# Two attention products in quarters of TensorE, and the delta rule's products on halves of the weight columns

## The chip, the cores and the metric

The program runs on one core of a Trainium2 chip. A time is the device time of one execution in microseconds (us). The matrix engine is TensorE, the others are VectorE, ScalarE and GpSimd; SyncE issues most of the DMAs. In the rows of the profile they are PE (with PEld for loads of weights), DVE, ACT, POOL and SP. A matrix product on TensorE loads weights of up to 128 rows by 128 columns and then streams up to 512 columns of the other operand past them, into one of eight PSUM banks of 128 partitions by 512 values.

## The reference, cut to what matters

All data are float32. A block of one model is followed by a block of another, on 1024 tokens of width 1024. The two parts that matter are the neighbourhood attention of the first block and the gated delta rule of the second.

```python
scores = jnp.einsum('bhrnqd,bhrnikd->bhrnqik', q_blk, kg).astype(jnp.float32)
scores = scores + bias[None]
scores = jnp.where(valid[:, :, None, :], scores, -1e30)
probs = jax.nn.softmax(scores, axis=(-2, -1)).astype(v.dtype)
out = jnp.einsum('bhrnqik,bhrnikd->bhrnqd', probs, vg)
...
t_mat = jnp.eye(CHUNK, dtype=jnp.float32) + bc[..., :, None] * dec_strict * kk
w_mat = lax.linalg.triangular_solve(t_mat, (bc * eG)[..., None] * kc, left_side=True, lower=True,
                                    unit_diagonal=True)
u_v = lax.linalg.triangular_solve(t_mat, bc[..., None] * vc, left_side=True, lower=True,
                                  unit_diagonal=True)
...
def step(S, xs):
    w_c, uv_c, qd_c, intra_c, kt_c, gl_c = xs
    u = uv_c - jnp.einsum('bhck,bhkv->bhcv', w_c, S)
    o = jnp.einsum('bhck,bhkv->bhcv', qd_c, S) + jnp.einsum('bhij,bhjv->bhiv', intra_c, u)
    S = jnp.exp(gl_c)[..., None, None] * S + jnp.einsum('bhck,bhcv->bhkv', kt_c, u)
    return S, o
```

The attention has 8 heads of width 64 on a grid of 16 rows by 64 tokens; a row attends to 8 rows, 512 keys. The delta rule has 8 heads of width 64, runs in both directions over 256 context tokens and then 1024 others.

## The kernel before, in words

Every engine has its own list of instructions, written out in order. They wait for each other through counters: each producer ticks one, and a consumer waits for a count. PSUM is a ring of eight banks (`Banks`): `bk.open(key, ...)` takes the next bank for a product, `bk.vacant` waits until its former content is gone, `bk.full` until it is filled, `bk.clear` until it is emptied. An order that is opened is the order in which the banks go round.

*First attention* (`tensor_natt`, `vector_natt`, `scalar_natt`, `gpsimd_natt`, L577 to L674). There are 64 items, one for a row of 64 tokens and a pair of heads j; head s of the pair lies on partitions 64s to 64s+63 of queries and keys. The queries `QB` are block-diagonal: an area of 128 partitions by 2 x 64 columns, zero where the head doesn't match, so that one product of 128 rows by 128 weight columns by 512 keys gives the scores of both heads (L591). VectorE adds the bias (L632) and takes the negative maximum (L636), ScalarE does the exponential with its sum (L659), VectorE the reciprocal (L641), GpSimd scales the row (L674), TensorE turns it in four transposes (L600), ScalarE copies that out of PSUM (L667), and TensorE multiplies it with the values, eight products with 64 weight columns, each head on its half of the output partitions (L617). VectorE copies the result out as a high and a low part (L647, L649). On TensorE item i's scores stand ahead of item i-3's transposes and item i-4's value products; ScalarE does the exponential of i and then the copy of i-3. Scores live in 2 buffers, exponentials in 5, turned ones in 3. The queries' copy from PSUM (`vector_query_out`, L512) is one instruction per head, and GpSimd zeroes `QB` beforehand (L559).

*Delta rule* (`tensor_delta` and its like, L2530 to L2640). It runs in rounds n of 128 tokens, dd being the direction. Each round's triangular matrices (8 heads, 2 directions) are inverted: diagonal blocks of 32 by 32 on VectorE in 30 steps (L2241, L2244), for round n+1 while round n's chain runs; out by DMA, one copy turned on ScalarE (L2252), and in again as `Y0` and `YT`. Blocks are then joined to 64 (`tensor_join_a`, L2286, `tensor_join_b`, L2309) and to 128 (`tensor_join_c` to `e`, L2330, L2348, L2366). The state's chain is: keys times state (`tensor_step_a`, L2388), residual on VectorE (L2398, L2400), the inverse times the residual (`tensor_step_b`, L2410), scaling on VectorE (L2418), queries times state (L2436), the state's product (`tensor_step_c`, L2445), output (`tensor_step_o`, L2458), the state's sum on VectorE (L2477). The next round's blocks of the matrix (L2176) leave by SyncE's DMAs (L2199) and return, half of them turned on ScalarE (L2220), before VectorE begins their inverse (L2237). In L2286, L2309, L2410 and L2458 the weights are 128 by 128 and 64 columns stream; in L2445 128 stream, of which the diagonal 64 by 64 parts are used. A float32 product is two instructions of weights and two of streaming.

## Time and profile before

| | |
|---|---|
| median of 3 runs | 3741.59 us (3739.25 to 3743.46) |
| the profiled execution | 3733.37 us, of which the span of instructions 3731.6 us |
| TensorE busy | 3562.2 us, 95% of the span |
| VectorE, ScalarE, GpSimd busy | 1847.5, 1186.6 and 704.0 us |
| granted TensorE clock, mean | 0.981 |
| first attention | about 165 to 322 us |
| delta rule, rounds | about 1936 to 2316 us |

A time in a row is from the start of the span. In a timeline a row is a run of like instructions of one engine: start, length of the run, engine, line, operation, operands, how many, and in brackets how long the engine was idle before it and what ended that. A granted clock of 1 is 2.4 GHz, 0.5 is 1.2 GHz.

### The profile page before, as it was taken

The numbers are of one execution on the slowest core, as the hardware profiler recorded it, in microseconds if no ns is written. First come the engines' busy times: TensorE is split into PE (matmuls) and PEld (weight loads), VectorE is DVE, ScalarE is ACT, GpSimd is POOL, SyncE is SP. The second block draws the span as 40 slices with busy tenths as digits, with TensorE's granted clock in tenths as the row PEclk, the third lists the DMA queues.
The fourth block names the chain that finished last, engine by engine and source line by source line (L and its number), as shares of the span: only waits on it lengthen the run. The fifth ranks groups of instructions, "written<-read, shape, count | busy, mean of one in ns | idle before, by whom it ended". The sixth has DMA issues, their size and how long they took to land. (4 is left out here: it accounts for less than half of the span.)

```text
span 3731.6 us, 46421 instructions
## 1 busy us (share of the span) xinstructions
PE 3562.2 (95%) x18318; PEld 2764.2 (74%) x18318; DVE 1847.5 (50%) x3351; ACT 1186.6 (32%) x2087; POOL 704.0 (19%) x532
## 2 busy tenths in 40 slices
PE   7999999999999999999988988988999999999998
PEld 6756778887888888875557877546788478888886
DVE  4276993213676555335578884669211142322322
ACT  3155772212311111234434553138211032111210
POOL 1163000010101111010020110129101113333333
PEclk9999999999999999999999998999999999999999
DMA  3100111112233232123012214000122111111111
GB/s 134 37 2 22 44 40 51 54 55 87 75 106 96 91 105 93 46 78 125 1 22 41 39 38 138 27 1 2 35 74 59 54 57 46 51 51 46 49 53 46
DMA packets 266342, 211.67 MB, mean 57 GB/s; under 512 B 65680, under 2 KB 231184, under 8 KB 265744
## 3 DMA queue, kind: packets, MB, share of 16 engines
q1 hardware_dynamic: 264368, 201.61, 17.4%
q10 hardware_dynamic: 1760, 7.08, 0.9%
q8 instruction: 149, 2.44, 0.3%
q14 instruction: 65, 0.53, 0.0%
HBM read 185.33 MB, written 21.50 MB: 55 GB/s over the span
## 5 line engine op out<-in xcount | busy, mean ns | idle before, releaser
L95 PE MATMUL ps<-halves 128*128 128x512 f32 x10408 | 2406.7, 392 | 19.1 <-DVE halves L1542 6.6
L95 PEld LDWEIGHTS ps<-halves 128*128 128x128 f32 x10408 | 1956.1, 188 | 441.4 <-issue 26.9
L95 PE MATMUL ps<-arena 128*128 128x512 f32 (+1 forms) x880 | 361.7, 564 | 11.2 <-issue 6.4
L1521 POOL TENSOR_TENSOR tmps<-tmps 128x512 f32<-128x512 f32 x128 | 143.7, 1123 | 981.4 <-ACT tmps L1489 981.4
L1542 DVE TENSOR_TENSOR halves<-tmps,halves 128x512 fp32r<-128x512 f32 x128 | 88.1, 691 | 435.4 <-ACT halves L1497 435.4
L1425 ACT ACTIVATE halves<-raws 128x2048 fp32r<-128x2048 f32 x62 | 118.3, 1909 | 556.0 <-PE ps L95 532.5
L95 PEld LDWEIGHTS ps<-arena 128*128 128x128 f32 x880 | 165.7, 193 | 170.3 <-issue 159.3
L1528 POOL TENSOR_TENSOR arena<-arena 128x512 f32<-128x512 f32 x128 | 164.8, 1294 | 191.3 <-DVE arena L1569 191.3
L1489 ACT ACTIVATE tmps<-ps 128x512 f32<-128x512 f32 x128 | 76.6, 598 | 363.9 <-PE ps L95 360.0
L1569 DVE TENSOR_TENSOR arena<-ps,arena 128x512 f32<-128x512 f32 x128 | 87.8, 690 | 194.9 <-PE ps L95 188.7
L1365 DVE SCALAR_TENSOR_TENSOR arena<-arena,sc 128x128 f32<-128x128 f32 x448 | 164.1, 366 | 15.9
L1432 DVE TENSOR_TENSOR halves<-raws,halves 128x2048 fp32r<-128x2048 f32 x62 | 142.0, 2290 | 55.3 <-ACT halves L1425 55.3
L95 PE MATMUL ps<-arena,tokens 128*128 128x512 f32 (+1 forms) x384 | 140.2, 523 | 0.0
L2943 POOL TENSOR_SCALAR arena<-arena,wst 128x640 f32<-128x640 f32 (+1 forms) x64 | 119.0, 1873 | 89.8 <-DVE wst L2897 89.7
L1559 DVE TENSOR_TENSOR arena<-arena,ps 128x512 f32<-128x512 f32 x128 | 85.2, 683 | 99.7 <-PE ps L95 99.7
L674 POOL TENSOR_SCALAR arena<-arena,sm 128x512 f32<-128x512 f32 x64 | 100.1, 1565 | 176.1 <-DVE sm L641 176.1
L2116 POOL TENSOR_TENSOR arena<-arena 128x512 f32<-128x512 f32 x40 | 44.5, 1140 | 455.0 <-PE ps L95 232.5
L1497 ACT ACTIVATE halves<-tmps 128x512 fp32r<-128x512 f32 x128 | 81.0, 633 | 154.5 <-POOL tmps L1521 154.5
L95 PEld LDWEIGHTS ps<-arena,tokens 128*128 128x128 f32 x384 | 72.4, 191 | 62.2 <-issue 59.2
L2244 DVE TENSOR_TENSOR arena<-arena 64x30 f32<-64x30 f32 (+5 forms) x300 | 103.9, 346 | 10.3
L2241 DVE TENSOR_TENSOR arena<-arena 64x30 f32<-64x30 f32 (+5 forms) x300 | 102.9, 343 | 10.0
L1093 POOL TENSOR_TENSOR valw<-valw,arena 128x512 f32<-128x512 f32 x8 | 14.0, 1748 | 444.3 <-DVE arena L1076 444.3
(306 smaller groups left out, 3532.3 us busy)
## 6 DMA issues: line engine op xcount, KB each, us to landing
raws<-in_w_ff SPq DMA_DIRECT2D x31, 1024.0 KB, 6.5
raws<-in_w_mlp SPq DMA_DIRECT2D x31, 1024.0 KB, 5.4
mixw<-in_w_in SPq DMA_DIRECT2D x56, 512.0 KB, 3.8
arena<-in_w_ada SPq DMA_DIRECT2D x48, 512.0 KB, 3.9
arena<-in_w_in SPq DMA_DIRECT2D x5, 2048.0 KB, 11.9
arena<-in_x SPq DMA_DIRECT2D x8, 1024.0 KB, 8.3
h_stash<-arena SPq DMA_DIRECT2D x1, 5120.0 KB, 30.0
inverses<-arena ACTq DMA_DIRECT2D x20, 256.0 KB, 2.9
```

The lines of the kernel that those rows point to most:

```text
L95: ins = e.matmul(out_ap, l, r, start=i == 0, stop=i == n - 1)
L674: e.tensor_scalar(pbuf[i % 5], pbuf[i % 5], c[:, 2:3], None, ALU.mult).then_inc(*a_sl.tick())
L1365: e.scalar_tensor_tensor(out=a, in0=raw_a[:, kk, :], scalar=sc3[:, kk, b:b + 1], in1=a, op0=ALU.mult, op1=ALU.add).then_inc(*(m_part if kk ...
L1425: e.activation(RR[:, FW + q * 4096:FW + q * 4096 + 2048], raw_of(n), ACT.Copy).then_inc(*f_wh.tick())
L1432: e.tensor_tensor(RR[:, FW + q * 4096 + 2048:FW + q * 4096 + 4096], raw_of(n), RR[:, FW + q * 4096:FW + q * 4096 + 2048].bitcast(F32), ALU ...
L1521: e.tensor_tensor(tt, tt, tt, ALU.mult).then_inc(*f_sq.tick())
L1528: e.tensor_tensor(dst, dst, tmg[(i * 8 + t) % 2], ALU.add).then_inc(*f_ad.tick())
L1542: e.tensor_tensor(fl[:, m, n0:n0 + N], ftmp[x % 2], fh[:, m, n0:n0 + N].bitcast(F32), ALU.subtract).then_inc(*f_fl.tick())
L1569: e.tensor_tensor(tmg[x % 2], bk.tile(key)[:, :], G2[:, nh * 512:nh * 512 + 512], ALU.mult).then_inc(*bk.emptying(key))
L2241: e.tensor_tensor(T3, bc(W3[:, k:k + 1, k + 1:32], [64, k, 31 - k]), bc(W3[:, 0:k, k:k + 1], [64, k, 31 - k]), ALU.mult).then_inc(*dv.tick())
L2244: e.tensor_tensor(W3[:, 0:k, k + 1:32], W3[:, 0:k, k + 1:32], T3, ALU.add).then_inc(*(i_sol if k == 30 else dv).tick())
L2943: ins = e.tensor_scalar(p, p, w4[i % 4][:, 6 + s:7 + s], None, ALU.mult)
```

## The change

- Scores are made for two items at a time. The queries hold no zeros any more; each head is a product of 64 rows by 64 weight columns by 512 keys. The four products of two items use the four quarters of the array: for even items head 0 goes to output partitions 0 to 63, for odd ones to 64 to 127 (`natt_rows`). The bias table's heads are swapped for odd j to match. The value products come 5 items behind instead of 4.
- The sum with the bias and the minimum of its negative are one `tensor_tensor_reduce`; ScalarE's exponential then has scale -1. VectorE's reciprocals and copy-outs go in pairs.
- The queries' copy from PSUM is one instruction for both heads; the two zero fills of `QB` are gone, and the copy waits for all eight scaled rows instead.
- The two joins of 32 to 64 are products of 32 by 32 by 32 on four quarters of 32 rows and 32 columns, one bank and one key for both directions. ScalarE copies the first one out in one instruction. Two zero fills of GpSimd go.
- L2410, L2458 and L2445 take 64 weight columns at a time, for the two halves of the output partitions; L2445 now makes the diagonal parts alone.

```diff
         def vector_query_out(e, m, h):
             key = ("q", m, h)
-            e.wait_ge(*q_zero.at(m // 2 + 1))
+            e.wait_ge(*n_xn.at(8))
             e.wait_ge(*bk.full(key))
-            for s in range(2):
-                rows = slice(64 * s, 64 * s + 64)
-                ins = e.tensor_scalar(
-                    QB[rows, m, 8 * h:8 * h + 8, s, :],
-                    bk.tile(key)[rows, :].rearrange("p (r q) -> p r q", q=64), V("bq", m)[rows], 0.125,
-                    ALU.add, ALU.mult)
-            ins.then_inc(*bk.emptying(key))
+            e.tensor_scalar(QB[:, m, 8 * h:8 * h + 8, 0, :], bk.tile(key)[:, :].rearrange("p (r q) -> p r q", q=64),
+                            V("bq", m), 0.125, ALU.add, ALU.mult).then_inc(*bk.emptying(key))
...
+        def natt_rows(i, s):
+
+            a = 64 * ((s + i) % 2)
+            return slice(a, a + 64)
+
         def tensor_natt(e):
-            for i in range(64 + 4):
-                if i < 64:
-                    r, j, start = natt_place(i)
-                    key = ("as", i)
-                    o = bk.open(key, a_ev)
-                    e.wait_ge(*bk.vacant(key))
+            for i in range(64 + 5):
+                if i < 64 and i % 2 == 0:
+                    for u in (i, i + 1):
+                        bk.open(("as", u), a_es)
+                        e.wait_ge(*bk.vacant(("as", u)))
...
-                    e.matmul(o[:, :], QB[:, j, r, :, :], KT[:, j, start * 64:start * 64 + 512], start=True,
-                             stop=True).then_inc(*bk.filling(key))
+                    for s in range(2):
+                        for u in (i, i + 1):
+                            r, j, start = natt_place(u)
+                            f = slice(64 * s, 64 * s + 64)
+                            ins = e.matmul(bk.tile(("as", u))[natt_rows(u, s), :], QB[f, j, r, 0, :],
+                                           KT[f, j, start * 64:start * 64 + 512], start=True, stop=True)
+                            if s == 1:
+                                ins.then_inc(*bk.filling(("as", u)))
...
-                if 0 <= i - 4 < 64:
-                    u = i - 4
+                if 0 <= i - 5 < 64:
+                    u = i - 5
...
-                    e.tensor_tensor(sb[i % 2], bk.tile(key)[:, :], BI[:, j, off * 64:off * 64 + 512],
-                                    ALU.add).then_inc(*bk.emptying(key))
-                    c = statn[:, i % 8, :]
-                    e.wait_ge(*bk.clear(key))
-                    e.tensor_reduce(c[:, 0:1], sb[i % 2], AX.X, ALU.max, negate=True).then_inc(*a_mx.tick())
...
+                    e.tensor_tensor_reduce(out=sb[i % 2], in0=bk.tile(key)[:, :], in1=BI[:, j, off * 64:off * 64 + 512],
+                                           scale=-1.0, scalar=3.0e38, op0=ALU.add, op1=ALU.min,
+                                           accum_out=statn[:, i % 8, 0:1]).then_inc(*bk.emptying(key))
+                for u in ((), (i - 1, i))[i % 2]:
+                    if u < 64:
+                        c = statn[:, u % 8, :]
+                        if u == i and i >= 5:
+                            vector_natt_out(e, i - 5)
+                        e.wait_ge(*a_ex.at(u + 1))
+                        e.reciprocal(c[:, 2:3], c[:, 1:2]).then_inc(*a_rc.tick())
+                if i >= 5 and (i % 2 == 0 or i >= 64):
+                    vector_natt_out(e, i - 5)
...
             for h in range(8):
-                ins = e.matmul(o[:, h * 64:h * 64 + 64], AT[n % 2][dd][:, h, :], Y0[dd][:, h, :], start=True, stop=True)
+                for dd, q in QUARTERS:
+                    first, second = blk32(FIRST(dd, q)), blk32(SECOND(dd, q))
+                    ins = e.matmul(o[second, h * 32:h * 32 + 32], AT[n % 2][dd][first, h, second], Y0[first, h, :],
+                                   start=True, stop=True)
             ins.then_inc(*bk.filling(key))
...
-            for q in range(2):
-                r = blk32(SECOND(dd, q))
-                ins = e.activation(PM[dd][r, :, blk32(FIRST(dd, q))], h8(bk.tile(key))[r, :, blk32(q)], ACT.Copy)
-            ins.then_inc(*bk.emptying(key))
...
+            e.activation(PM, q8(bk.tile(key)), ACT.Copy).then_inc(*bk.emptying(key))
...
             for h in range(8):
-                ins = e.matmul(o[:, h * 64:h * 64 + 64], PM[dd][:, h, :], y[:, h, :, 1 - dd, :], start=True, stop=True)
+                for dd, q in QUARTERS:
+                    first, second = blk32(FIRST(dd, q)), blk32(SECOND(dd, q))
+                    ins = e.matmul(o[first, h * 32:h * 32 + 32], PM[second, h, :], YT[n % 2][dd][second, h, second],
+                                   start=True, stop=True)
             ins.then_inc(*bk.filling(key))
...
             for h in range(8):
-                ins = e.matmul(o[:, h * 64:(h + 1) * 64], YT[n % 2][dd][:, HEAD(h), :], rb_[dd][:, h, :], start=True,
-                               stop=True)
+                for a in BOTH:
+                    ins = e.matmul(o[half(a), h * 64:(h + 1) * 64], YT[n % 2][dd][:, HEAD(h), half(a)], rb_[dd][:, h, :],
+                                   start=True, stop=True)
             ins.then_inc(*bk.filling(key))
...
             for j in range(4):
-                ins = e.matmul(o[:, j * 128:(j + 1) * 128], kt[:, ORDERS[dd][n], j * 128:(j + 1) * 128],
-                               rb_[dd][:, 2 * j:2 * j + 2, :], start=True, stop=True)
+                for s in BOTH:
+                    f = j * 128 + s * 64
+                    ins = e.matmul(o[half(s), j * 64:(j + 1) * 64], kt[:, ORDERS[dd][n], f:f + 64],
+                                   rb_[dd][:, 2 * j + s, :], start=True, stop=True)
             ins.then_inc(*bk.filling(key))
...
             for h in range(8):
-                ins = e.matmul(o[:, h * 64:(h + 1) * 64], IT[n % 3][dd][:, HEAD(h), :], ub_[dd][:, h, :],
-                               start=True, stop=True)
+                for a in BOTH:
+                    ins = e.matmul(o[half(a), h * 64:(h + 1) * 64], IT[n % 3][dd][:, HEAD(h), half(a)], ub_[dd][:, h, :],
+                                   start=True, stop=True)
             ins.then_inc(*bk.filling(key))
```

## Rows read from the trace of the kernel before

**Rows 1.** Busy time by stretch: stretch, length, each engine (instructions), clock, DMA.
```profile
184.00:316.00 132.00, 123.05 (x1243) 77.55 (x1243) 101.35 (x283) 73.70 (x171) 88.98 (x57) 1.00 0.01 2
325.00:640.00 315.00, 315.00 (x1276) 239.48 (x1275) 229.25 (x190) 183.98 (x216) 0.00 (x0) 1.00 0.16 44
```

**Rows 2.** Timeline of one item of the first attention, TensorE and ScalarE's copy.
```profile
202.07 1.12 PE L591 MATMUL ps<-arena 128*128 128x512 f32 x2
...
203.04 0.60 PE L600 MATMUL ps<-identm,arena 128*128 128x128 f32 x4
...
203.13 0.58 ACT L667 ACTIVATE arena<-ps 128x512 f32<-128x512 f32 x1
...
203.85 0.69 PE L617 MATMUL ps<-arena 128*64 128x64 f32 x16 [0.22 <-ACT arena L667]
...
204.47 1.13 PE L591 MATMUL ps<-arena 128*128 128x512 f32 x2
```

**Rows 3.** Timeline of a steady delta round: VectorE, ScalarE, ScalarE's DMA queue.
```profile
2133.96 0.09 DVE L2237 MEMSET arena<- 64x32 f32 x1 [1.16 <-ACT arena L2220]
...
2153.43 1.27 DVE L2418 TENSOR_TENSOR arena<-ps,arena 128x512 f32<-128x512 f32 x2
...
2158.76 0.45 ACTq L2251 DMA_DIRECT2D inverses<-arena  x1
...
2169.28 2.04 ACT L2220 ACTIVATE arena<-arena 32x1024 f32<-32x1024 f32 x1 [1.73 <-DMA arena<-blocks]
...
2171.48 0.09 DVE L2237 MEMSET arena<- 64x32 f32 x1 [1.42 <-ACT arena L2220]
```

**Rows 4.** Timeline of TensorE in the same round.
```profile
2141.15 1.15 PE L2330 MATMUL ps<-identm,arena 64*64 64x64 f32 x32
...
2148.21 3.76 PE L2410 MATMUL ps<-arena 128*128 128x64 f32 x32
```

**Rows 5.** Timeline of TensorE in the second attention, scores of one item.
```profile
2526.78 1.35 PE L2807 MATMUL ps<-arena 64*128 64x384 f32 x8
```

**Rows 6.** Groups of instructions by line: count, busy us, mean ns, idle before.
```profile
L632 DVE TENSOR_TENSOR arena<-ps,arena 128x512 f32<-128x512 f32 x64 | 44.2, 691 | 29.6 <-PE ps L591 17.8 <-ACT arena L659 11.8
...
L636 DVE TENSOR_REDUCE sm<-arena 128x1 f32<-128x512 f32 x64 | 43.9, 686 | 2.2
...
L659 ACT ACTIVATE arena<-arena,sm 128x512 f32<-128x512 f32 x64 | 46.2, 722 | 68.0 <-DVE sm L636 68.0
...
L659 ACT ACTIVATION_READ_ACCUMULATOR arena<-arena,sm 128x1 f32 x64 | 11.9, 187 | 0.0
...
L822 DVE TENSOR_TENSOR_SCAN arena<-arena 128x1024 f32<-128x1024 f32 x16 | 36.7, 2291 | 0.5
```

**Rows 7.** Timeline of VectorE before the first attention: a copy of queries.
```profile
35.64 1.51 DVE L512 TENSOR_SCALAR arena<-ps,vec 64x512 f32<-64x512 f32 x2 [2.91 <-PE ps L95]
```

**Rows 8.** Timeline of the last delta rounds: TensorE, VectorE, ScalarE's and SyncE's DMAs.
```profile
2264.15 7.06 PE L2410 MATMUL ps<-arena 128*128 128x64 f32 x32 [1.38 <-ACT arena L2374]
...
2267.84 0.69 DVE L2418 TENSOR_TENSOR arena<-ps,arena 128x512 f32<-128x512 f32 x1 [2.56 <-PE ps L2410]
2271.25 0.69 DVE L2418 TENSOR_TENSOR arena<-ps,arena 128x512 f32<-128x512 f32 x1 [2.72 <-PE ps L2410]
...
2276.19 0.45 ACTq L2251 DMA_DIRECT2D inverses<-arena  x1
...
2283.53 3.90 SPq L2275 DMA_DIRECT2D arena<-inverses  x8
...
2287.13 3.74 PE L2286 MATMUL ps<-arena 128*128 128x64 f32 x32
...
2295.39 1.15 PE L2330 MATMUL ps<-identm,arena 64*64 64x64 f32 x32 [0.94 <-ACT arena L2317]
...
2301.76 5.55 PE L2410 MATMUL ps<-arena 128*128 128x64 f32 x32 [1.38 <-ACT arena L2374]
...
2312.24 3.68 PE L2458 MATMUL ps<-arena 128*128 128x64 f32 x32
```

More of the change, by code:

```diff
@@ L2314, in scalar_join_b @@
             e.wait_ge(*bk.full(key))
[L2315 removed]
+            for dd, q in QUARTERS:
                 r = blk32(FIRST(dd, q))
[L2317 removed]
+                ins = e.activation(YT[n % 2][dd][r, :, blk32(SECOND(dd, q))], q8(bk.tile(key))[r, :, :], ACT.Copy)
             ins.then_inc(*bk.emptying(key))
```

103 lines of the change are left out of this document (43 added, 60 removed).

## The prediction

> **What bounds the kernel now.** I read the engine shares first: TensorE is busy 95% of the span, so what counts is where it is not, and where it runs slower than it could. The diff touches two stages, and the sums of busy time by stretch [rows 1] say how full the engines are around the first. In the first attention (184 to 316 us) 57 items pass in 132 us, 2.32 us an item: TensorE is busy 123 us of it, VectorE 101, GpSimd 89. Then the timeline of one attention item [rows 2]: the score product starts at 202.07, the transposes at 203.04, the value products at 203.85 after 0.22 us of waiting for ScalarE's copy, and the next score product at 204.47. TensorE does 0.97 us of scores and 1.21 us of the rest (1.25 in the sums below, so as not to reckon too tightly); what is left up to 2.32 is that wait, in some items more and in some none. So TensorE bounds this stage, with ScalarE's copy close behind it. From 325 to 640 us TensorE is busy 315 of 315 us [rows 1], so what is won before reaches the end.
>
> The delta rule looks alike and isn't. In a round of its steady part [rows 3] VectorE starts its inverse at 2133.96 and has the blocks solved at 2158.76, which ScalarE's DMA shows. Through two DMA trips and a turning copy on ScalarE (2169.28, after 1.73 us of waiting for the blocks' DMA) the next inverse starts at 2171.48. That is 24.80 + 12.72 = 37.52 us, and nothing in it waits for TensorE: the inverse's output product L2410 began at 2148.21 and took 3.76 us [rows 4], 1.46 us before VectorE came for it at 2153.43. TensorE has work for most of the round, but this loop sets the round.
>
> **The change, part by part.**
>
> *Scores in quarters.* Now one product of 128 rows by 128 weight columns an item: 0.97 us to the transposes behind it. After: four products of 64 by 64 for two items, each still with 512 columns moving. Alone each takes as long as the old one, 0.97 us; all depends on how many run at once. The trace has two at once, both ways: sixteen value instructions on column halves in 0.69 us [rows 2], and eight 64-row products of the second attention (four of 384 columns, four of 256) in 1.35 us [rows 5]. One after the other the latter would take, at the scores' 0.97 us for 2 x 512 columns, (4 x 384 + 4 x 256) x 0.97/1024 = 2.4 us. The transposing products L2330, 32 on two diagonal quarters, take 1.15 us [rows 4]: 0.036 us each, some 0.03 without the last one's own length, against 3.76/32 = 0.118, some 0.11, for full-width weights. Four at once is shown nowhere. Bounds: 0.97 us a pair of items (four at once) and 3.9 (one at a time). I take 0.97, since rows and columns each overlap fully and the four quarters are distinct. A pair then costs TensorE 0.97 + 2 x 1.25 + 0.15 for one more change of tile shape (an estimate, below the 0.22 us between the transposes' end and the value products' start) = 3.6 us, 1.8 us an item.
>
> The Trainium skill speaks against this. TensorEngine Tiling (Array Packing), section Restrictions and Gotchas, says that different row tiles cannot access the same PSUM bank simultaneously; each bank of a pair is here filled by both row halves. The trace disagrees: L2330 writes both of its row halves into one bank and still goes at 0.036 us or less. By the page the quarters would go two at a time; that is rival 1.
>
> *Sum and minimum in one VectorE instruction.* Goes: the sum of 0.691 and the maximum of 0.686 us [rows 6]. Comes: one fused instruction, in no row. It reads 512 columns once, so nearest is one pass, 0.69; the dearer bounds are 0.69 + 0.187, if its accumulator is read as ScalarE's is [rows 6]; 1.15, at the rate of the scan, 2291 ns for 1024 columns [rows 6]; and 1.37, both old passes. I take 0.8. Is TensorE still the bound? VectorE's other work is 101.35/57 - 0.691 - 0.686 = 0.40 us an item. In a pair it now waits for the second exponential (0.722 + 0.187 = 0.91 us) before its reciprocal, with one item's other work ahead of that: 2D + 0.40 + 0.91 + some 0.1 of handing over = 2D + 1.41, which is 3.0 us at D = 0.8. The chain through ScalarE is fused instruction, exponential, copy, exponential: 0.8 + 0.91 + 0.58 + 0.91 = 3.2 and a reciprocal. GpSimd's scaling is 88.98/57 = 1.56 an item, 3.12. All three stay under 3.6 by little. The stage: 63 x (2.32 - 1.8) = 33 us; less 3 because four engines are now within 0.5 us of each other, and a jitter in one shows. **-30 us.** The values come one item later than before (5 instead of 4 behind the scores); the first one waits for the DMA of shifted values as before, so this is hidden, and would cost one item's 1.8 us otherwise.
>
> *Two zero fills of queries and the second copy-out.* GpSimd's fills were off the path. VectorE's two 64-row copies (1.51 us a pair [rows 7]) become one of about 0.69; one such pair stands right before the split that TensorE waits for. **-0.6 us** (0 to -0.8). The stricter wait, for all eight scaled rows, stands on VectorE behind those very rows: nothing.
>
> *Joins, outputs and state products.* Full-width weights cost 0.11 to 0.12 us an instruction, half-width ones on two halves some 0.03 [rows 2, 4]. Per round the inverse's output goes from 32 instructions to 64: 3.6 to 1.9 us. Both joins alike, 3.6 to 1.9 each (64 instructions of 32 by 32; taken at the same 0.03, bounds 0.015 and 0.06: from one half of it, as the columns are halved too, to no overlap between directions). The two outputs -1.7 together, the state product -0.85. That is 7.7 us of TensorE a round, 77 in ten. In the steady rounds all of it lies beside VectorE's loop: **0 us**. The cover is the 1.46 us of slack above, which grows. ScalarE copies the first join once instead of four times, and waits for a DMA afterwards anyway. The DMAs are as many as before and wait for the same. The fewer fills before the first round are hidden: the fill of the states waits for other work.
>
> *The last rounds* have no loop beside them, and TensorE is on the path [rows 8]. (a) Round 8: VectorE waits 2.56 and 2.72 us for L2410, which takes 7.06 us at half clock, started late by a join at half clock. Both waits go: -5. (b) From the last solution (2276.19) to the first join (2287.13), 10.94 us with two outputs in it, then bounded by the DMA that brings the inverses: -1. (c) First join to L2330, 8.26 us: two joins save 3.4, but one key for both directions ends the overlap of one direction's copy with the other's product, and the eight DMAs issued from 2283.53 for 3.90 us land near 2289.3, before which the second join cannot start: -1.5. (d) From 2301.76 to 2312.24 + 3.68 = 2315.92: L2410 5.55 to 2.5 (part of it at half clock), state product -0.85, outputs 3.68 to 2.0: -5.5. **-13 us.**
>
> Sum: -30 - 0.6 - 13 = -43.6 us. The profiled execution took 3733.4 us, so 3689.8 of its kind; it was 8.2 us below the median of the runs shown, 3741.6, and I predict for that: **3698.0 us**. Within it, the forecast runs from -36 to -54 us (3688 to 3706): D up to 0.9, the last rounds between -8 and -18.
>
> **The rivals.** (1) *Quarters two at a time* (by the page's rule above, or a shared way for the moving data): 2 x 0.97 + 2.65 = 4.6 us a pair, 2.3 an item, the attention gives 1 us, total -14.6: 3727. Against it: L2330. 10%. (2) *The fused instruction costs both passes*, D = 1.37: 2D + 1.41 = 4.15 a pair, 2.08 an item, attention -15, total -29: 3713. For it: it isn't in the trace at all. The Trainium skill, DVE: opcode table, instruction layouts, handler registers and perf-mode slots, section 6. Datapath and trigger behaviour, says that a stage which reads its own last result runs without a bubble and that the scan runs at half rate; the scan's row bears the second out, and no row here shows the first. 10%. (3) *The clock.* With 7.7 us less work a round TensorE idles longer in steady rounds, and half clock came after such idling in rounds before. L2410 took 7.06 us in round 8 [rows 8] against 3.76. If the clock were half from L2330 (2141.15) to the end of L2410 (2151.91), these 10.8 us, 9.1 after the change, would be 18.2; the slack of 1.46 grows by 1.7 from L2410 and by 1.1 from the join, to 4.3, so VectorE would wait 4.8 us in each of 7 rounds: +34, total -10: 3732. Half of it at half clock would cost nothing. Against it: the stretch is dense. 4%. (4) *Slower: the quarters don't overlap.* 4 x 0.97 + 2.65 = 6.5 us a pair, 3.27 an item, attention +60, total +46: 3788. The sign turns where the four take more than 2.4 us together (an item over 2.54, so that the attention loses the 13.6 us that the rest gives). Against it: both kinds of halves overlap in the trace. 4%.
>
> **How the numbers follow.** Forecast 72%, rivals 10, 10, 4 and 4. The range leaves out (3), (4), most of (1) and the forecast's lower tail: 3683 to 3723. 0.2% is 7.5 us, about what a measurement can tell from no change. Faster 0.93, same 0.03, slower 0.04.
>
> **What would show it.** In the changed profile a pair of attention items should take 3.5 to 3.8 us, the four quarters' eight instructions should start within two groups 0.43 us apart, and the fused instruction should take 0.7 to 0.9 us. Steady delta rounds should still be 37 to 38 us apart with TensorE less busy and VectorE still waiting for ScalarE's turning copy. The last round should lose VectorE's two waits for L2410, and L2410 should take near 2 us. A fused instruction over 1.2 us, quarters that start one behind the other, or a steady round over 38.5 us would make the prediction wrong.

## The result, and the profile after

The changed kernel takes 3680.8 us (median of 4 runs, 3678.4 to 3684.2), against 3740.4 us for the kernel before in the same comparison (4 runs, 3739.2 to 3743.5): a ratio of 0.984, 95% interval 0.9823 to 0.9857. That is 59.6 us, where I had forecast 43.6; the time is 2.2 us below the low end of my range, 3683. The profiled execution of the changed kernel has a span of 3677.7 us, 53.9 us less than that of before.

I cut both spans at the same five events: the first score product; the first product behind the attention; the first state product of the delta rule; the start of VectorE's last inverse; and the first product behind the delta rule. Each number is a difference of two start times in the timeline, in us. ("The start of VectorE's last inverse" is its `MEMSET`, L2237 before and L2244 after.)

| stretch | before | after | difference | predicted |
|---|---|---|---|---|
| to the first score product | 165.09 | 163.25 | -1.84 | -0.6 |
| attention | 156.99 | 117.03 | -39.96 | -30 |
| to the first state product | 1613.89 | 1611.22 | -2.67 | 0 |
| steady delta rounds | 311.65 | 311.68 | +0.03 | 0 |
| last rounds | 68.13 | 57.93 | -10.20 | -13 |
| the rest | 1415.81 | 1416.62 | +0.81 | 0 |

The attention, in the sums by stretch from 184 to 266 us (columns: length, busy time and instructions of TensorE, its weight load, VectorE, ScalarE and GpSimd, granted clock, DMA share, GB/s), to be set beside [rows 1]:

```profile
184.00:266.00 82.00, 82.00 (x1152) 51.30 (x1152) 58.37 (x241) 62.27 (x144) 74.30 (x49) 1.00 0.01 2
```

TensorE is busy the whole of it and no other engine is. The timeline of one pair of items, which answers to [rows 2] (start, duration, engine, line, operation, the program's names, shapes):

```profile
196.01 1.09 PE L591 MATMUL ps<-arena 64*64 64x512 f32 x8
...
197.03 0.66 PE L602 MATMUL ps<-identm,arena 128*128 128x128 f32 x4
197.16 0.69 DVE L634 CUSTOM_DVE_ANT_0 arena<-ps,arena 128x512 f32<-128x512 f32 x1
...
197.62 0.69 PE L619 MATMUL ps<-arena 128*64 128x64 f32 x16
197.77 0.08 DVE L634 DVE_READ_ACCUMULATOR2_ANT sm<- 128x1 f32 x1
...
198.24 0.66 PE L602 MATMUL ps<-identm,arena 128*128 128x128 f32 x4
...
198.82 0.69 PE L619 MATMUL ps<-arena 128*64 128x64 f32 x16
...
199.44 1.09 PE L591 MATMUL ps<-arena 64*64 64x512 f32 x8
```

A pair takes 199.44 - 196.01 = 3.43 us. Four quarter products of 512 columns hold TensorE for 1.02 us, hardly more than one full product did (0.97). They start in two groups: four of their eight instructions by 196.05, all eight by 196.52. The fused instruction takes 0.69 us and 0.08 for its accumulator.

The steady delta rounds take the same time in sum, but they are less even. From inverse to inverse the last seven of them take 36.33, 38.69, 36.81, 38.85, 36.27, 38.81 and 37.36 us, in the mean 37.6; before, they took 36.21 to 38.39, in the mean also 37.6. VectorE still waits for ScalarE's turning copy ahead of most of them. The last rounds, TensorE's timeline, which answers to [rows 8] (L2396, L2297, L2317, L2419, L2445, L2456 and L2470 are what L2388, L2286, L2309, L2410, L2436, L2445 and L2458 were; a bracket gives the idle time ahead and what ended it):

```profile
2217.26 3.68 PE L2419 MATMUL ps<-arena 128*64 128x64 f32 x64 [1.38 <-ACT arena L2382]
...
2231.78 3.75 PE L2396 MATMUL ps<-arena 128*128 128x128 f32 x16 [6.22 <-DVE arena L2489]
2235.46 1.31 PE L2470 MATMUL ps<-arena 128*64 128x64 f32 x32
2236.70 0.75 PE L2297 MATMUL ps<-arena 32*32 32x32 f32 x64
2240.40 1.07 PE L2317 MATMUL ps<-arena 32*32 32x32 f32 x64 [2.94 <-DMA arena<-inverses]
2243.21 1.97 PE L2338 MATMUL ps<-identm,arena 64*64 64x64 f32 x32 [1.73 <-ACT arena L2326]
2245.96 1.98 PE L2356 MATMUL ps<-arena 64*64 64x64 f32 x32 [0.78 <-ACT arena L2346]
...
2252.06 3.68 PE L2419 MATMUL ps<-arena 128*64 128x64 f32 x64 [1.38 <-ACT arena L2382]
```

The output of the inverse takes 3.68 us for 64 instructions, still at half clock, where it took 7.06 for 32 in round 8 of before. From the last round's first join (2236.70) to the state product (2255.68) TensorE's waits are 7.6 of 19.0 us.

So two things were to be explained: a larger gain in the attention, and some 6 us more between the medians than between the two profiled executions.

### The profile page after: what moved, and what is told of

The parts are those of the page before. It is cut to its first block and busy times, and to the rows that moved or that the text cites. A ratio compares the mean times of both kernels' runs of the same rounds, so it can differ in the third digit from the quotient of the medians.

```text
span 3677.7 us, 49398 instructions
## 1 busy us (share of the span) xinstructions
PE 3455.9 (94%) x19822; PEld 2656.2 (72%) x19822; DVE 1802.4 (49%) x3343; ACT 1175.1 (32%) x2057; POOL 693.2 (19%) x528
## 5 line engine op out<-in xcount | busy, mean ns | idle before, releaser
L1429 ACT ACTIVATE halves<-raws 128x2048 fp32r<-128x2048 f32 x62 | 118.4, 1909 | 554.8 <-PE ps L95 532.4
L95 PEld LDWEIGHTS ps<-arena 128*128 128x128 f32 x880 | 165.9, 193 | 168.4 <-issue 157.3
```

Of the source, the lines that this page charges most:

```text
L95: ins = e.matmul(out_ap, l, r, start=i == 0, stop=i == n - 1)
L1429: e.activation(RR[:, FW + q * 4096:FW + q * 4096 + 2048], raw_of(n), ACT.Copy).then_inc(*f_wh.tick())
```

## The experiments

Each ratio is against runs of the kernel before on the same chip. I name the kernels by their edit.

**The attention's part alone**, and **the delta rule's part alone**: the kernel before with one group of the hunks each.

> The kernel before with the attention's part of the change alone: one query copy-out, no zero fills of queries, quartered scores two items at a time, the fused instruction, values five items behind. My reading of the two traces (the parts add up, none leans on another): -42 us against before, of it -40 between the first score and the end of the stage and -1.8 ahead of it; a pair of items every 3.42 us; the fill of the states and the last delta rounds as before (68.3 us from the last round's first inverse step on). Rival, that part of what the delta rounds gained comes from the attention's new layout or from a shift in time: the last rounds get shorter here too, by some 3 us or more.

> The kernel before with the delta rule's part of the change alone: joins of 32 by 32 quarters, 64 weight columns on halves in the inverse's, output and state products, two fills less. My reading: -13 us, of it -2.7 ahead of the first delta step (GpSimd has 3.3 us less of fills before the gates that the decay rows wait for), 0 in the steady rounds and -10.4 in the last rounds. Rival, the steady rounds do gain or lose where nothing covers them up (the clock, a queue): more than 2 us off -13, and the distance from the first state step to the last inverse is not 311.7 us.

The attention alone takes 3705.5 us (3692.9 to 3708.3), ratio 0.9887 (0.9857 to 0.9918) to 3743.6. That is -42.3 us by the ratio (0.0113 x 3743.6), with an interval of -31 to -54, and -38.1 between the medians; both fit the -42 I expected. Its attention takes 118.67 us. The delta rule alone takes 3722.9 us (3717.2 to 3723.4), ratio 0.994 (0.9919 to 0.9962): -22.5 us by the ratio and -20.7 between the medians, in place of -13, although its own stretches are what I expected: 311.84 us of steady rounds, 57.54 in the last rounds, 1611.86 ahead of the first state product. The two together give 65 us by the ratios and 58.8 between the medians, the whole 59.6; they add up within their intervals. But the attention's kernel, whose delta rule is that of before, shows what I had not: its steady rounds take 319.67 us, not 311.65. One of them takes 43.36 us, where the three profiles of before (table below) have 36.21, 38.50 and 38.35. In TensorE's timeline of that kernel (its L2290 and L2313 are the joins L2286 and L2309):

```profile
1942.67 3.75 PE L2392 MATMUL ps<-arena 128*128 128x128 f32 x16 [6.84 <-DVE arena L2481]
1947.52 7.06 PE L2290 MATMUL ps<-arena 128*128 128x64 f32 x32 [1.09 <-DVE arena L2402]
...
1956.62 6.92 PE L2313 MATMUL ps<-arena 128*128 128x64 f32 x32
```

and in the sums by stretch of the same kernel, from 1948 to 1966 and the 18 us behind it:

```profile
1948.00:1966.00 18.00, 18.00 (x77) 15.28 (x78) 11.35 (x35) 6.21 (x14) 0.00 (x0) 0.51 0.09 13
1966.00:1984.00 18.00, 15.33 (x214) 12.98 (x208) 13.20 (x35) 8.65 (x19) 0.00 (x0) 1.00 0.13 26
```

Behind a wait of 6.84 us TensorE's clock is granted at 0.51 from 1948 to 1966, which is 1.2 GHz; both full-width joins fall into that and take 14 us. VectorE then waits for TensorE inside the inverse:

```profile
1969.27 1.29 DVE L2180 SCALAR_TENSOR_TENSOR arena<-ps,arena 128x512 f32<-128x512 f32 x2 [6.24 <-PE ps L2352]
```

That is the mechanism of my third rival, in a kernel with the old joins. But the wait by itself doesn't decide it. In the profile from which I predicted, the same round has the same wait, and the clock was up again within the first join:

```profile
1977.48 3.75 PE L2388 MATMUL ps<-arena 128*128 128x128 f32 x16 [6.86 <-DVE arena L2477]
1981.03 4.42 PE L2286 MATMUL ps<-arena 128*128 128x64 f32 x32
...
1987.00 3.76 PE L2309 MATMUL ps<-arena 128*128 128x64 f32 x32 [0.40 <-DMA arena<-inverses]
```

So with full-width joins the time of a round varies with how long the half clock lasts; what makes it last longer in one execution than in another, no run here shows.

**The fused instruction alone**, with the scores of before:

```diff
-                    e.tensor_tensor(sb[i % 2], bk.tile(key)[:, :], BI[:, j, off * 64:off * 64 + 512],
-                                    ALU.add).then_inc(*bk.emptying(key))
-                    c = statn[:, i % 8, :]
-                    e.wait_ge(*bk.clear(key))
-                    e.tensor_reduce(c[:, 0:1], sb[i % 2], AX.X, ALU.max, negate=True).then_inc(*a_mx.tick())
+                    e.tensor_tensor_reduce(out=sb[i % 2], in0=bk.tile(key)[:, :], in1=BI[:, j, off * 64:off * 64 + 512],
+                                           scale=-1.0, scalar=3.0e38, op0=ALU.add, op1=ALU.min,
+                                           accum_out=statn[:, i % 8, 0:1]).then_inc(*bk.emptying(key))
...
```

> The kernel before with the fused sum-and-minimum instruction alone, its scores still full-width products one item at a time. If TensorE bounds an item (0.97 + 1.21 = 2.18 us of the 2.32, the rest a wait for ScalarE's copy that a shorter VectorE chain takes away), an item takes 2.18 to 2.25 us and the time falls by 5 to 9 us. Rival, that VectorE's chain set the old rhythm and the fused instruction is what won most of the 40 us: an item under 2.0 us, -20 us or more.

3726.5 us (3720.2 to 3746.2, 10 runs), ratio 0.9961 (0.9943 to 0.9979): -14.6 us by the ratio, -17.1 between the medians. The stage takes 144.42 us, 12.6 less than before, more than the 5 to 9 expected. TensorE is busy without a gap (112.00 of 112.00 us from 184 to 296), and its timeline shows how it spends 2.10 us on an item:

```profile
199.75 1.12 PE L591 MATMUL ps<-arena 128*128 128x512 f32 x2
...
200.71 0.60 PE L600 MATMUL ps<-identm,arena 128*128 128x128 f32 x4
...
201.24 0.69 PE L617 MATMUL ps<-arena 128*64 128x64 f32 x16
...
201.85 1.13 PE L591 MATMUL ps<-arena 128*128 128x512 f32 x2
```

0.96 + 0.53 + 0.61 us. The transposes and values cost 1.14 us, not the 1.21 I read or the 1.25 I reckoned with. I had misread the wait in [rows 2]. Its bracket of 0.22 us counts from the end of the transposes' row, 0.60 us long; here a row of that length is followed by the value products 0.53 us after its start. So the wait was 0.81 - 0.53 = 0.28 us, and the transposes cost 0.53 and not 0.59.

The same kernel's last delta rounds take 81.50 us, where the profile that I predicted from has 68.13 with the same code:

```profile
2281.67 7.04 PE L2284 MATMUL ps<-arena 128*128 128x64 f32 x32
2288.50 7.03 PE L2307 MATMUL ps<-arena 128*128 128x64 f32 x32
2296.48 1.97 PE L2328 MATMUL ps<-identm,arena 64*64 64x64 f32 x32 [0.94 <-ACT arena L2315]
```

These are L2286 and L2309 of before; there the first of the last round's joins began at 2287.13 and L2330 8.26 us later [rows 8], here L2328 begins 14.81 us after the first join. The granted clock is 0.50 from 2281 to 2296. TensorE's wait ahead of that round's L2386 was 2.63 us, against 2.67 ahead of L2388 before: again like waits, and another clock. This profile is of an execution of 3737.9 us, 11.5 above the median of its kernel, so its last rounds are not the usual ones.

**The quartered scores with the sum and the maximum apart**: the changed kernel, its fused instruction undone as in the diff above.

> The changed kernel with the fused instruction taken apart again into a sum and a maximum, as before, beside the quartered scores. By the sum of the prediction, 2D + 1.41 with D = 0.691 + 0.686, a pair takes 4.15 us instead of 3.42: +23 us against after. Rival, TensorE bounds the pair whatever VectorE does: within 3 us of after. Second rival, the chain is longer than my sum has it: over 4.4 us a pair, +30 or more.

3703.1 us (3700.7 to 3705.7), ratio 0.9883 (0.9869 to 0.9898), some 20 above the changed kernel, and the attention takes 137.75 us, 20 more. I had expected 23. TensorE's score products start 4.08 us apart, the next at 207.42:

```profile
199.26 1.09 PE L592 MATMUL ps<-arena 64*64 64x512 f32 x8
203.34 1.09 PE L592 MATMUL ps<-arena 64*64 64x512 f32 x8
```

The sum 2D + 1.41 gave 4.15. So VectorE's chain was rightly priced, and with D = 0.69 + 0.08 = 0.77 it comes to 2.95 us a pair, below TensorE's 3.42. Beside the 157.3 us that the attention takes before, the quarters with two passes bring 19.5 us, the fused instruction alone 12.8, and both together 39: some 7 us come only where both are there, because quarters with two passes end on VectorE.

**The step products alone**: the kernel before with 64 weight columns on halves in the inverse's, output and state products; joins and fills as before.

```diff
-                ins = e.matmul(o[:, h * 64:(h + 1) * 64], YT[n % 2][dd][:, HEAD(h), :], rb_[dd][:, h, :], start=True,
-                               stop=True)
+                for a in BOTH:
+                    ins = e.matmul(o[half(a), h * 64:(h + 1) * 64], YT[n % 2][dd][:, HEAD(h), half(a)], rb_[dd][:, h, :],
+                                   start=True, stop=True)
```

> The kernel before with 64 weight columns on halves in the inverse's, output and state products alone; joins and fills stay as before. My steps a, b and d hold these: -5 for the two waits in round 8, half of b, -5.5 at the end, so -10 to -11 expected then, joins -1.5 to -2.5 more. As the whole gave 10.4, this one should give 8 to 9, all of it in the last rounds, and the joins the rest. Rival, the joins carry the last rounds, since they sit in the serial chain at half clock: this kernel gives 5 or less.

3728.2 us (3722.6 to 3734.9, 10 runs), ratio 0.9951 (0.9936 to 0.9966): -18.3 us by the ratio and -15.3 between the medians, about twice the 8 to 9 I had expected. Its last rounds take 58.73 us, 9.4 less than in the first profile of before, as expected, so the rest of the gain is not there; part of it shows in the steady rounds of the table below. With the joins (the delta rule's part alone) the last rounds take 57.54. So the joins bring 1.2 us there. Why so little, when they save 3 us each: in this kernel the clock is up from the last round's joins on,

```profile
2289.00 3.79 PE L2286 MATMUL ps<-arena 128*128 128x64 f32 x32
2292.62 3.74 PE L2309 MATMUL ps<-arena 128*128 128x64 f32 x32
2297.30 1.15 PE L2330 MATMUL ps<-identm,arena 64*64 64x64 f32 x32 [0.94 <-ACT arena L2317]
2299.23 1.15 PE L2348 MATMUL ps<-arena 64*64 64x64 f32 x32 [0.78 <-ACT arena L2338]
...
2303.68 2.09 PE L2411 MATMUL ps<-arena 128*64 128x64 f32 x64 [1.38 <-ACT arena L2374]
```

while in the changed kernel the same three products take 1.97, 1.98 and 1.98 us and the output of the inverse 3.68 (above). The short joins are 3.79 + 3.74 - 0.75 - 1.07 = 5.7 us shorter, but the second one now waits 2.94 us for its DMA, so that from the first join to the product behind both it is 6.51 us instead of 8.30, 1.8 less. The half clock behind them takes back 0.82 + 0.83 + 0.83 + 1.59 = 4.1. What the joins gain comes from the round before, whose second join takes 6.49 us here and 1.08 with quarters: in the changed kernel the last round's first join starts 33.52 us after the start of the last inverse, here 36.54.

**The two fills back**: the changed kernel with the fills of 2048 and 1024 columns where they stood.

```diff
             e.memset(R(12288, 4096), 0.0).then_inc(*s_zero.tick())
+            e.memset(R(16384, 2048), 0.0).then_inc(*s_zero.tick())
+            e.memset(R(18432, 1024), 0.0).then_inc(*s_zero.tick())
             gpsimd_gates(e, 1, 1)
...
```

> The changed kernel with the two fills of 2048 and 1024 columns back on GpSimd, between the gates of the second group and behind the first fill, where they stood before. If the decay rows ahead of the first delta step wait for the gates behind these fills, +2.7 to +3.3 us against the kernel after, and TensorE's idle time ahead of that decay row goes from 3.4 to 6.4 us. Rival, that the fills are hidden, as I predicted: 0, and the 2.7 us came from something else that changed ahead of it.

3685.3 us (3683.6 to 3687.8), ratio 0.9836 (0.9822 to 0.9851): too close to the changed kernel's to tell 3 us by the runs. The row tells it. TensorE's timeline ahead of the second decay rows, with the fills,

```profile
1888.76 2.05 PE L95 MATMUL ps<-arena 128*128 128x512 f32 x2 [6.43 <-issue]
```

and in the changed kernel without them,

```profile
1882.07 2.04 PE L95 MATMUL ps<-arena 128*128 128x512 f32 x2 [3.36 <-issue]
```

3.07 us of TensorE's time come and go with the fills, which took 1.80 and 1.49 on GpSimd; in the kernel before the same product (at 1927.18) waited 6.44. Most of it reaches the first state product: from the product ahead of that wait it is 19.04 us with the fills and 16.30 without. My rival, hidden fills, is out.

**The kernel before profiled twice more, and the changed kernel again.**

> The kernel before, unchanged, profiled again. Its profile shown first was 8 us faster than the median of its runs. If that profile was of an execution in which the last delta rounds ran at a kinder clock than they mostly do (68.1 us there, 81.5 in the kernel with the fused instruction alone, whose delta rule is the same), this one has 70 us or more in the last rounds, or a steady round of 40 us or more. Rival, the 8 us lie elsewhere, in the long stages behind: 68 us in the last rounds, 311.7 in the steady ones, and a longer last stage than 1415.8.

> The same as the one ahead of it, a third profile of the kernel before, to see how its last delta rounds and its steady rounds vary: 68 to 82 us and 312 to 320 us expected, longer than the changed kernel's by 10 to 23 us in the last rounds and by 0 to 8 in the steady ones. Rival, as there.

> The changed kernel once more, unchanged, on the chip of the next three, for its stages and the spread of its runs. In the runs so far the kernels with full-width products in the delta rule spread widely (before 3732 to 3759 in 19 runs, with the fused instruction alone 3720 to 3746 in 10) and those with narrow ones less (3678 to 3684). If the changed kernel's TensorE has room in the steady delta rounds, its runs again lie within 7 us, the distance from the first state step to the last inverse is 311 to 313 us and the last rounds take 58 us. Rival, the narrow spread was chance: runs 15 us or more apart.

The two take 3745.5 and 3742.5 us; the changed kernel takes 3683.3 (3675.9 to 3685.3), ratio 0.9838 (0.9821 to 0.9856). Its spread is 9.4 us, a little above the 7 I had set. The last rounds of the second profile of before, 72.07 us, are in what I had expected, those of the third, 67.73, are shorter; its steady rounds, 316.09, are inside. By stretches, all profiled executions, in us:

| kernel | step products | steady rounds | last rounds |
|---|---|---|---|
| before, three profiles | full width | 311.65, 315.51, 316.09 | 68.13, 72.07, 67.73 |
| attention alone | full width | 319.67 | 68.47 |
| fused instruction alone | full width | 313.28 | 81.50 |
| delta rule alone | narrow | 311.84 | 57.54 |
| step products alone | narrow | 312.04 | 58.73 |
| after, two profiles | narrow | 311.68, 311.58 | 57.93, 58.28 |
| fills back | narrow | 310.95 | 58.10 |
| two passes | narrow | 311.55 | 57.87 |
| transposes and values in pairs (below) | narrow | 311.12 | 57.91 |

The five profiles with full-width step products have 315.2 us in the mean for the steady rounds and 71.6 for the last ones; those with narrow ones (the kernels with idle products, below, left out) lie within 1.1 and 1.2 us. The 71.6 leans on the one profile of 81.50; the other four have 69.1. The first profile of before, from which I predicted, had the shortest steady rounds of the five. Part of the rest is the clock, as above. Another part shows in the third profile of before, where VectorE comes to the last but one of these inverses without waiting for its blocks:

```profile
2207.36 3.52 PE L2458 MATMUL ps<-arena 128*128 128x64 f32 x16
...
2213.34 2.04 ACT L2220 ACTIVATE arena<-arena 32x1024 f32<-32x1024 f32 x1 [1.48 <-DMA arena<-blocks]
...
2215.39 1.28 DVE L2499 TENSOR_TENSOR arena<-arena,ps 128x512 f32<-128x512 f32 x2
...
2216.64 0.09 DVE L2237 MEMSET arena<- 64x32 f32 x1
```

The blocks are turned at 2215.38, but VectorE is in the sum L2499, which needs both output products, of which one took 3.52 us (the other 1.90). In the repeated profile of the changed kernel the output product is done earlier and the inverse waits for its blocks again:

```profile
2166.34 1.15 PE L2470 MATMUL ps<-arena 128*64 128x64 f32 x32
2167.94 1.28 DVE L2511 TENSOR_TENSOR arena<-arena,ps 128x512 f32<-128x512 f32 x2
...
2171.29 0.09 DVE L2244 MEMSET arena<- 64x32 f32 x1 [2.07 <-ACT arena L2227]
```

How often each of the two happens in a run, and what else lengthens the rounds of 38.4 and 38.5 us, I did not trace. The kernel with the step products alone still has joins of 6.93 us, at half clock, in its second and third rounds and yet 312.04 us of steady rounds. That narrow step products keep the rounds short is what seven profiles against five say; by which of the two ways they do it is not shown.

**Idle products in TensorE's waits**: the changed kernel, products that nobody reads in front of the real ones of the last two rounds.

```diff
+        def tensor_busy(e, o, k):
+            for _ in range(k):
+                e.matmul(o[:, :], ident[:, :], kT[:, 0, 0:512], start=True, stop=True)
...
         def tensor_join_b(e, n):
             key = ("lt", n)
             o = bk.open(key, e_ea)
             e.wait_ge(*bk.vacant(key))
+            tensor_busy(e, o, BUSY.get(key, 0))
...
```

> The changed kernel with idle products (identity by keys, 512 columns, into a bank that the next real product overwrites) where TensorE waits in the last two delta rounds: 6 and 4 ahead of the second joins, 2, 1 and 1 ahead of the later joins, 8 ahead of the last round's first state product. If the half clock of these rounds comes from TensorE's waits, and the products there are on the path, the clock stays up and products such as the inverse's output take 2.1 instead of 3.7 us: -6 to -10 us against after. Rivals: the clock stays at half all the same (+0 to +3, the idle products delay the real ones), or it rises but the chain through ScalarE and the DMAs takes the gain (0 to -2).

3681.7 us (3678.0 to 3684.1), ratio 0.9825 (0.9811 to 0.984), not to be told from the changed kernel, where I had expected 6 to 10 us. But the last rounds take 55.04 us, 3 less, and the clock came up as the expectation's first case has it: the sums by stretch have 1.00 from 2236 on. The real products are faster, and the idle ones delay the first of them:

```profile
2232.07 7.84 PE L2310 MATMUL ps<-arena,identm 128*128 128x512 f32 x16
2239.75 1.95 PE L2409 MATMUL ps<-arena 128*128 128x128 f32 x16
...
2257.30 2.08 PE L2432 MATMUL ps<-arena 128*64 128x64 f32 x64 [1.39 <-ACT arena L2393]
```

The product of the inverse's output takes 2.08 us, not 3.68. But eight idle products started at a lower clock (0.81 from 2232 to 2236) and took 7.84 us in a wait that was 6.22. So in the last round of the changed kernel the clock stays up where products fill TensorE's waits; how far that pays depends on the fit.

**Transposes and values in pairs**: the changed kernel, two transposes, then two value products, with the copy-outs two items later.

```diff
-            for i in range(64 + 5):
-                if i < 64 and i % 2 == 0:
+            for i in range(0, 64 + 6, 2):
+                if i < 64:
...
-                if 0 <= i - 3 < 64:
-                    u = i - 3
+                for u in (i - 4, i - 3):
+                    if not 0 <= u < 64:
+                        continue
                     key = ("at", u)
...
-                if 0 <= i - 5 < 64:
-                    u = i - 5
+                for u in (i - 6, i - 5):
+                    if not 0 <= u < 64:
+                        continue
```

> The changed kernel with the transposes of two items back to back and then the value products of two items, in place of one of each in turn: three changes of tile shape a pair instead of five. If a change costs TensorE about 0.1 us beside the work itself, a pair goes from 3.42 to 3.2 us, where GpSimd's scaling, 3.12, is next: -5 to -7 us. Rivals: changes of shape cost nothing (0 us), or the transposes come too late for ScalarE's copies and the pair gets longer than 3.42 (slower).

3669.2 us (3666.2 to 3673.7), ratio 0.9797 (0.978 to 0.9813), faster than both kernels; the attention takes 106.43 us, 10.6 less than the first profile after, more than I expected.

```profile
201.33 1.09 PE L591 MATMUL ps<-arena 64*64 64x512 f32 x8
...
202.35 1.09 PE L603 MATMUL ps<-identm,arena 128*128 128x128 f32 x8
...
203.37 1.15 PE L621 MATMUL ps<-arena 128*64 128x64 f32 x32
...
204.45 1.09 PE L591 MATMUL ps<-arena 64*64 64x512 f32 x8
```

A pair takes 3.12 us: 1.02 + 1.02 + 1.08. Two transposes and two value products together cost 2.10 us, against 2.41 one after the other (197.03 to 199.44 above): two changes of tile shape less, 0.15 us each. The kernel with the fused instruction alone agrees: 2 x 1.14 = 2.28 us there, with one change less than 2.41, 0.13 us. That it is the change of shape, and nothing else in the order, no run tests by itself. GpSimd is now busy 71.78 of 72.00 us from 184 to 256, with 1.56 us an item, and is the other bound.

**Both, the idle products cut to fit**: pairs as above; idle products of 256 columns in the last round alone (10 ahead of the first state product, then 6, 3, 1, 1 and 2).

> The changed kernel with transposes and value products grouped by pairs, as in the grouped kernel before it, and with idle products in the last delta round alone, in units of 256 columns that should fit its waits (10 ahead of the first state product, 6, 3, 1, 1 ahead of the joins, 2 ahead of the inverse's output). The grouping gave 10.6 us of the attention; in the kernel with longer idle products the clock stayed up through both last rounds, but they overran three waits by 1.4, 0.7 and 0.3 us and round 8 was set by VectorE's inverse, so that 2.9 us were left. Here: last rounds 53 us instead of 58, so -15 us against the kernel after. Rival, the clock doesn't come up within one round of idle products: 58 us or more in the last rounds, -10.

3668.2 us (3667.7 to 3669.8, 5 runs), ratio 0.9802 (0.9787 to 0.9818). The last rounds take 53.65 us, 4.3 less than with pairs alone (57.91), nearly the 5 expected. The time is that of the pairs alone: its comparison was another one, and 1.0 us between the medians is less than either interval, so these runs don't show the 4.3 us. In the profile the stretch ahead of the first state product takes 1612.42 us against 1608.87 with pairs alone, with the same code: 3.6 us the other way. -15 us against after was expected, and -15.1 is what the medians of the last comparison give (3683.3 to 3668.2).

## Why the prediction was right or wrong

The sum by steps, with means over the profiled executions of kernels that share the code of a stretch: -1.5 to the first score product (166.0 in six, 164.5 in eight; both scatter by 4 us), -38.9 in the attention (157.3 in five, 118.4 in five), -3.6 ahead of the first state product (1615.9 in seven, 1612.3 in seven), -3.8 in the steady rounds, -13.5 in the last ones, +0.9 behind. That is -60.4 us, beside -59.6 between the medians. I had -43.6. Without the one profile of 81.50 us the last rounds give -11.1, the steady ones -4.2, and the sum is -58.4.

**The query copies, right.** Much of the scatter in the first stretch is the clock: its two groups of 48 products take 11.2 us each at full clock, and 12.8 in executions where the granted clock falls within them (0.72 from 42 to 46 us in the first profile of before), in kernels of either kind. What the change does is in TensorE's wait ahead of the second group: 3.57 or 3.58 us in six profiles with two copies, 3.11 or 3.12 in eight with one, -0.46. I had -0.6. Beside it, with the fills gone GpSimd's sum L556 begins at 24.12 and not at 34.91, and VectorE's L327, at 29.11, takes 6.25 us instead of 2.74; that fills the 2.91 us for which VectorE waited in [rows 7].

**Quarters, right, and by the row rather than by the Trainium skill.** All four ran at once: 1.02 us for four, where I took 0.97 for the forecast and 1.94 for rival 1. The Trainium skill, TensorEngine Tiling (Array Packing), Restrictions and Gotchas, says that different row tiles cannot access the same PSUM bank simultaneously; each bank here is filled by both row halves, each on partitions of its own, and the trace disagrees, in L591 as it did in L2330. Rivals 1 and 4 are out.

**The attention's size, wrong by 9 us, more than half of the miss.** Two terms of the sum failed. The step "TensorE does 0.97 us of scores and 1.21 us of the rest (1.25 in the sums below, so as not to reckon too tightly)" was mis-sized: with no wait in it the rest is 1.14. 2 x 0.11 less 0.05 for the slower scores makes a pair 3.43 us instead of 3.6, and 31 pairs some 5.5 us. A pair is thus below the 3.5 to 3.8 us that I had named as the sign. The 0.15 for one more change of tile shape was right, by the kernel with pairs. The other is "less 3 because four engines are now within 0.5 us of each other": there is no jitter to be seen, TensorE is busy 82.00 of 82.00 us. It was a margin, and I booked it as a cost.

**The fused instruction, right.** 0.69 + 0.08 = 0.77 us, against 0.8 taken; rival 2 (1.37) is out, and the kernel with two passes shows that what I said it would cost, 4.15 us a pair, it does (4.08). The sentence of the Trainium skill that I had cited in its favour (DVE: opcode table, instruction layouts, handler registers and perf-mode slots, 6. Datapath and trigger behaviour: a stage that reads its own last result runs without a bubble) fits that row.

**"The fewer fills before the first round are hidden", wrong, 3.1 us.** I looked at the last fill of the states, ahead of the first state product, which does wait for other work. The gates between the fills do not, and TensorE's decay rows wait for them. The step that failed is that I asked who waits for the fills and not who waits for what is queued behind them on GpSimd.

**"In the steady rounds all of it lies beside VectorE's loop: 0 us", wrong for the runs, right for the profile.** I read the round in which nothing waits for TensorE and took it for all rounds. In the profile that I read the narrow products change nothing there. Against the mean of five profiles they save 3.8 us, and 8 against one execution whose joins ran at half clock. My rival 3 had a mechanism that exists, in the kernels with full-width products: I feared that less work would bring half clock into steady rounds; it was already there now and then, and with narrow step products no profile has a long sum of rounds. I had also named a steady round over 38.5 us as a sign of being wrong. Three rounds of the changed kernel are longer, up to 38.85, but so are rounds of the second and third profiles of before, and the sum is the same; a single round was no good sign.

**Last rounds, right in the parts, short by one term, and right in the mean by luck.** Against the profile that I read it was 10.2 us where I had 13. My parts came out so, between the events that I had named: (a) from the start of the last inverse to the last solution 28.57 to 23.20, -5.4 against -5; (b) 10.94 to 10.32, -0.6 against -1; (c) 8.26 to 6.51, -1.8 against -1.5; (d) -4.9 against -5.5. What I had at nothing is the stretch between (c) and (d): the products L2330, L2348 and L2366 went from 1.15 to 1.97 and 1.98 us each, at half clock, and L2410 began 8.85 us after L2330 instead of 6.37, +2.5. In the mean over the profiles it is 13.5, near my 13, because the full-width kernels lose more there than the one that I read; 2.5 of that is the single profile of 81.50 us. That agreement is luck.

**The anchor.** I saw that the profiled execution was 8.2 us below its median and set the difference off as if it had nothing to do with the change. It had: 3.6 us of the mean steady rounds and 3.4 of the mean last rounds are what distinguishes the first profile of before from the mean of its kind, and the change removes them. That is 7 of the 8 us; by the three profiles of before alone it is 2.8 and 1.2, 4 of the 8. Where it lies between the two, so few profiles can't say.

## What to carry to other kernels

Where a profiled execution is faster than the median of its runs, ask which stretch of it varies and whether the change touches that stretch; more profiles of the same kernel answer it. Margins belong in the range and not in the sum. Products of like tile shape back to back were worth 10 us here, and a fill on GpSimd costs whatever the work queued behind it makes others wait.

## What the runs showed of the hardware

- Four 64 by 64 quarters with 512 columns each, two of them writing the two halves of one PSUM bank and two another, hold TensorE for 1.02 us, one 128 by 128 product for 0.96.
- 64 products of 32 by 32 take 0.75 us at full clock, some 0.01 us each; I had put 0.015 as the lower bound.
- A change of tile shape seems to cost TensorE 0.15 us here, by two orders of the same products that differ in two such changes, and 0.13 by another pair of kernels.
- Shorter products can cost clock: with full-width joins in the last round the three products behind them took 1.15 us each in four of six profiles, and 1.97 or 1.98 in all six with quartered joins and no idle products. In the changed kernel TensorE had waited 6.22 and 2.94 us ahead of them.
- Like waits of TensorE are followed by half clock of unlike length: behind 6.84 and 6.86 us the two joins took 7.06 and 6.92 us in one execution, 4.42 and 3.76 in another.
- GpSimd beside VectorE: while GpSimd's output sum and the sums L2116 behind it run (to 2220.64), VectorE's first inverse steps take 0.70 to 1.19 us instead of about 0.2. It is so in the first profile of before and in the changed kernel as well. The third profile of before, timeline:

```profile
2216.15 2.49 POOL L2512 TENSOR_TENSOR arena<-arena 128x512 f32<-128x512 f32 x2 [3.15 <-DVE arena L2499]
...
2217.49 1.19 DVE L2244 TENSOR_TENSOR arena<-arena 64x30 f32<-64x30 f32 x1
...
2220.75 0.24 DVE L2241 TENSOR_TENSOR arena<-arena 64x84 f32<-64x84 f32 x1
```
